# Expert rows filed by running order, and the first half of them loaded and summed during the last blocks: an encoder layer on one Trainium2 core

## The reference

```python
lg = xt @ w_rg + b_rg;  g_sel = top-1 group of 4           # 4 groups of 8 experts
le = xt @ w_re[g_sel] + b_re                               # scores of the 8 experts of that group
pe_top, e_sel = lax.top_k(softmax(le), 2)
gate = pg_top * pe_top / sum(pe_top)                       # two gates for each token
h = silu(xb @ w1[e]) * (xb @ w3[e])                        # xb: the token's normalised row
y = (h @ w2[e]) * gate
x = x + y_first + y_second                                 # both experts of a token
out = rmsnorm(x, final_norm_g)
```

## Time and profile before

| | |
|---|---|
| median of 3 runs | 1198.32 us (1197.93 to 1200.55) |
| span of the profiled execution | 1197.2 us |
| TensorE busy | 1093.9 us, 91% |
| VectorE, ScalarE, GpSimd busy | 520.2, 400.4, 190.7 us |
| moved by DMA | 308.89 MB, mean 258 GB/s |
| from the last block's store to the end | 1159.04 to 1197.2 us |

### The profile page before, as it was taken

The page is one execution under the profiler, slowest core; times in us unless marked ns, Lnnn a source line. Parts: engine busy times, 40 slices in busy tenths (PEclk is TensorE's granted clock), DMA queues, the critical chain, the costliest instruction groups (busy, mean ns, idle before and its releaser), DMA issues.

```text
span 1197.2 us, 15506 instructions
## 1 busy us (share of the span) xinstructions
PE 1093.9 (91%) x5142; PEld 659.8 (55%) x5142; DVE 520.2 (43%) x893; ACT 400.4 (33%) x629; POOL 190.7 (16%) x236
## 2 busy tenths in 40 slices
PE   5999999999999999999968999999998898999960
PEld 4888888888866667878854333333332333333320
DVE  5741512111038897463363535352443343341518
ACT  5421323222135665112214242424143324233232
POOL 0110011010100000000001323232323333231210
PEclk9999999999999999999987999999998999998985
DMA  8733331711350005557368899999999999999536
GB/s 305 282 122 116 114 123 44 292 57 45 139 210 12 1 1 176 176 192 306 123 270 353 353 421 420 419 420 419 421 415 420 421 420 420 419 420 419 218 157 258
DMA packets 69248, 308.89 MB, mean 258 GB/s; under 512 B 9024, under 2 KB 9152, under 8 KB 43872
## 3 DMA queue, kind: packets, MB, share of 16 engines
q1 hardware_dynamic: 56144, 273.86, 57.4%
q0 software_dynamic: 13072, 34.63, 7.5%
HBM read 278.57 MB, written 39.06 MB: 265 GB/s over the span
## 4 chain that ended last, share of the span: by engine, by line
PE 69%; DMA 15%; DVE 9%; ACT 3%; issue 3%; SPq 0%; DVEq 0%; ACTq 0%; POOLq 0%; POOL 0%
PE ps L872 18%; PE ps L584 13%; PE ps L585 13%; PE ps L586 13%; DMA rawe<-in_w 11%; PE ps L899 7%; DMA x_scratch<-x 2%; PE ps L862 1%; DVE cur13b L1671 1%; ACT prob L1003 1%; PE ps L881 1%; DVE att L1376 1%; DVE mx L1356 1%; DVE mx L1355 1%; DMA ya<-y_scratch 1%
## 5 line engine op out<-in xcount | busy, mean ns | idle before, releaser
L584 PE MATMUL ps<-whi,xTh 128*128 128x512 f32 x480 | 187.8, 391 | 14.0 <-DVE wlo L1231 14.0
L585 PE MATMUL ps<-wlo,xTh 128*128 128x512 f32 x480 | 187.5, 391 | 0.0
L586 PE MATMUL ps<-whi,xTl 128*128 128x512 f32 x480 | 187.4, 391 | 0.0
L872 PE MATMUL ps<-cur13a,xT 128*64 128x512 f32 x656 | 159.3, 630 | 2.0 <-DVE xT L1648 1.6
L1671 DVE COPY cur13a<-rawe 128x4096 f32 x31 | 71.1, 2294 | 189.1 <-DMA rawe<-in_w 119.7
L872 PE MATMUL ps<-cur13b,xT 128*64 128x512 f32 x656 | 147.8, 592 | 0.0
L899 PE MATMUL ps<-cur,hT 128*64 128x512 f32 x640 | 146.2, 598 | 0.0
L1200 ACT ACTIVATE cur<-rawe 128x4096 f32 x31 | 112.1, 3617 | 3.7 <-issue 1.4
L969 ACT ACTIVATE zst<-ps,rstd 128x512 f32<-128x512 f32 x60 | 40.8, 687 | 204.4 <-PE ps L586 198.0
L584 PEld LDWEIGHTS ps<-whi,xTh 128*128 128x128 f32 x480 | 90.6, 189 | 33.0 <-issue 14.0
L585 PEld LDWEIGHTS ps<-wlo,xTh 128*128 128x128 f32 x480 | 90.7, 189 | 18.8
(11 more groups left out here) (212 smaller groups left out, 1384.1 us busy)
## 6 DMA issues: line engine op xcount, KB each, us to landing
rawe<-in_w SPq DMA_DIRECT2D x96, 2048.0 KB, 25.9
raw<-in_w_in SPq DMA_DIRECT2D x20, 1024.0 KB, 8.0
z_scratch<-zst POOLq DMA_DIRECT2D x60, 256.0 KB, 2.3
gat<-z_scratch SPq DMA_DIRECT2D x12, 512.0 KB, 3.9
xn_scratch<-rrow POOLq DMA_DIRECT2D x6, 1024.0 KB, 5.6
ya<-y_scratch SPq DMA_DIRECT2D x6, 1024.0 KB, 10.8
raw<-in_w_out SPq DMA_DIRECT2D x4, 1024.0 KB, 6.8
xcol<-in_x_cols SPq DMA_DIRECT2D x6, 512.0 KB, 10.2
```

Of the source, the lines that this page charges most:

```text
L584: pe.matmul(out, ah, bh, start=first, stop=False)
L585: pe.matmul(out, ah, bl, start=False, stop=False)
L586: return pe.matmul(out, al, bh, start=False, stop=last)
L872: mm = pe.matmul(ps[0][u * CAP:(u + 1) * CAP, :], xT[:, c, h * CAP:(h + 1) * CAP], cur13[h][:, :, c * 512 + u * 256:c * 512 + u * 256 + 25 ...
```

## The change

The two rows of a token are filed by the order in which its experts run: `slote` holds the smaller and the larger of the two places, so k = 0 is the expert that runs first. The gates are put in the same order. A third number, `nb - 4`, is computed. SP, after the load of `x2t`, reads that number, waits until so many stores have landed, and loads the k = 0 rows of 128 tokens each (512 KB each) to five buffers `ye` beside `gf`; the sixth reuses the first buffer and waits until VectorE has used it (`s_c1`). VectorE adds these rows to `x2t` right after its loop over blocks (`combine_first`). After `s_md` SP loads only the k = 1 rows, and `combine` has one instruction instead of two.

```diff
+    slote = small("slote", [P, 2, NT])
-    nbi = small("nbi", [1, 2], I32)
+    nbi = small("nbi", [1, 3], I32)
...
-    ya = [at(f"ya{t}", RAW_O + t * 8 * KB, [P, 2, D]) for t in range(NT)]
+    ya = [at(f"ya{t}", RAW_O + t * 4 * KB, [P, D]) for t in range(NT)]
+    ye = [at(f"ye{s}", (124 + 4 * s) * KB, [P, D]) for s in range(5)]
...
             sp.dma_start(x2t[:, :, :], x2_d.rearrange("(t p) d -> p t d", p=P)).then_inc(s_x2l, 16)
+            early = sp.value_load(nbi[0:1, 2:3], min_val=NE - 4, max_val=NB - 4)
+            sp.wait_ge(s_ys, 16 * early)
             sp.dma_start(gf[:, :], A["final_norm_g"].rearrange("(a n) -> a n", a=1).partition_broadcast(P)[:, 0, :]).then_inc(s_gf, 16)
+            for t in range(NT):
+                if t == 5:
+                    sp.wait_ge(s_c1, 1)
+                sp.dma_start(ye[t % 5][:, :], y_d[t * P:(t + 1) * P, 0, :]).then_inc(s_g0[t], 16)
             sp.wait_ge(s_md, 1)
             for t in range(NT):
-                sp.dma_start(ya[t][:, :, :], y_d[t * P:(t + 1) * P, :, :]).then_inc(s_g1[t], 16)
+                sp.dma_start(ya[t][:, :], y_d[t * P:(t + 1) * P, 1, :]).then_inc(s_g1[t], 16)
...
-            link(dve.tensor_copy(sloti[:, :, :], slotf[:, :, :]))
+            dve.tensor_tensor(slote[:, 0, :], slotf[:, 0, :], slotf[:, 1, :], ALU.min)
+            link(dve.tensor_tensor(slote[:, 1, :], slotf[:, 0, :], slotf[:, 1, :], ALU.max))
+            link(dve.tensor_copy(sloti[:, :, :], slote[:, :, :]))
...
+            dve.tensor_scalar(nbi[:, 2:3], ends[0:1, NE - 1:NE], 1.0 / CAP, -4.0, ALU.mult, ALU.add)
...
-            link(dve.reciprocal(gates[:, 0, :], v6[:, 7, :]))
-            link(dve.tensor_tensor(gates[:, 1, :], gates[:, 0, :], v6[:, 3, :], ALU.mult))
+            link(dve.reciprocal(v6[:, 4, :], v6[:, 7, :]))
+            dve.tensor_tensor(v6[:, 0, :], slotf[:, 0, :], slotf[:, 1, :], ALU.is_lt)
+            dve.tensor_tensor(v6[:, 1, :], slotf[:, 0, :], slotf[:, 1, :], ALU.is_ge)
+            link(dve.tensor_tensor(v6[:, 5, :], v6[:, 4, :], v6[:, 3, :], ALU.mult))
+            for k in range(2):
+                dve.tensor_tensor(gates[:, k, :], v6[:, 4, :], v6[:, k, :], ALU.mult)
+                link(dve.tensor_tensor(v6[:, 6, :], v6[:, 5, :], v6[:, 1 - k, :], ALU.mult))
+                link(dve.tensor_tensor(gates[:, k, :], gates[:, k, :], v6[:, 6, :], ALU.add))
...
+            def combine_first(t):
+                dve.wait_ge(s_g0[t], 16)
+                dve.scalar_tensor_tensor(out=x2t[:, t, :], in0=ye[t % 5][:, :], scalar=gates[:, 0, t:t + 1],
+                                         in1=x2t[:, t, :], op0=ALU.mult, op1=ALU.add).then_inc(s_c1, 1)
...
             def combine(t):
                 dve.wait_ge(s_g1[t], 16)
-                link(dve.scalar_tensor_tensor(out=x2t[:, t, :], in0=ya[t][:, 0, :], scalar=gates[:, 0, t:t + 1],
-                                              in1=x2t[:, t, :], op0=ALU.mult, op1=ALU.add))
-                dve.scalar_tensor_tensor(out=x2t[:, t, :], in0=ya[t][:, 1, :], scalar=gates[:, 1, t:t + 1],
+                dve.scalar_tensor_tensor(out=x2t[:, t, :], in0=ya[t][:, :], scalar=gates[:, 1, t:t + 1],
                                          in1=x2t[:, t, :], op0=ALU.mult, op1=ALU.add).then_inc(s_c2, 1)
...
             dve.wait_ge(s_x2l, 16)
+            for t in range(NT):
+                combine_first(t)
+            dve.wait_ge(s_c1, NT)
```

More of the change, by code:

```diff
@@ L363, in hybrid_layer @@
         s_g1 = [sem(f"s_g1{t}") for t in range(NT)]
+        s_g0 = [sem(f"s_g0{t}") for t in range(NT)]
+        s_c1 = sem("s_c1")
         s_c2 = sem("s_c2")
```

## The result

The changed kernel takes 1192.82 us (median of 5, 1192.00 to 1194.07), the kernel before in the same session 1198.94 us (5 runs, 1197.93 to 1200.55). The ratio is 0.9948 (0.9936 to 0.9960): 6.1 us faster. I had forecast 1190.7 and 7.6 us. The profiled execution has a span of 1191.0 us and was itself measured at 1192.82 us, so 1.8 us lie outside the span.

A forecast was written before the change was run, and what follows sets the result against it. It saw the weight stream at 415 to 421 GB/s mid-loop and 35.7 us without block work at the end. 1197.2 - 9.3 + 1.1 + 0.6 = 1189.6 us span, plus 1.1 gives 1190.7; range 1188.6 to 1193.6.

The forecast's parts named there:

- the two rivals at 1192.4 and 1192.6: TensorE's first product: another low-clock stretch, 1192.4, chance 0.07; last but one store: waits for three or four additions, 1192.6, 0.08.
- The early loads and additions: During the last block: six loads and additions hidden, ending about 1156 us; without that cover they would cost 7.2 us.
- my rival for a late wait: Early loads on SP: the wait passes only with the last store, so loads queue behind it; 1200.1 us, chance 0.03.
- The end, -9.3: After the last store: fourth tile's addition 5.4 us earlier, one addition fewer on three tiles saves 3.96; bounds 8.6 to 10.1.
- the shorter pieces are no slower: Loads after the last store: 512 KB in 4 KB rows keeps the pace of `x2t`, 1.39 us each.
- The gates, +1.1: Ahead of the first block: eight more gate instructions delay it, all paid at the end; 1.1 us, bounds 0.8 to 1.4.
- the traffic that stops near 680 us: Early loop: DMA nearly dry (41 GB/s) while SP waits for ScalarE's w2 copy, so a late block delays stream and end.
- The minimum and maximum of the places, 0: Ahead of the first gather: 0.28 us more, hidden behind the later gates; 0.3 us if that cover were gone.
- GpSimd held by the early additions, +0.6: Last but one store: early VectorE additions hold GpSimd's index copy and indirect DMA; 0.6 us late, from 0 to 2.5.
- the copy and one further addition are waited for: Last but one store: these waits make it land about 1158 us, 0.6 to 1.0 us late.
- Outside the span, 1.1: Whole execution: the median of the runs lies 1.1 us above the profiled span.
- The rival on the clock: TensorE's first product: longer idle time brings another 3.4 us at half clock, losing 1.7 us; 1192.4 us, chance 0.07.

The follow-up runs named there:

- e2_late_loads: Changed kernel with the loads of the k = 0 rows also waiting for the last store, so nothing is loaded or added early: 1199.72 us.
- e4_k_major: Changed kernel with both scratch tensors laid out [k, token, 1024], so each load's rows lie one behind the other: 1191.37 us.
- e6_pairs: Changed kernel with the k = 1 rows loaded in three loads of 1 MB instead of six of 512 KB, same places in memory: 1193.12 us.
- e1_front_only: Changed kernel with filing and gates in running order, but everything loaded and added after the last store as before: 1199.61 us.
- e9_no_reorder: Changed kernel without the eight instructions that put the gates in running order, so gates can go to wrong rows: 1190.42 us.
- e10_warm: Changed kernel with one extra unused TensorE product behind the turning of the rows of block 0 and of block 1: 1189.59 us.
- e11_best_warm: Changed kernel with gate instructions behind the first columns' copy, scratch laid out [k, token, 1024], and two extra unused TensorE products: 1188.95 us.
- e3_gates_later: Changed kernel with all 13 gate instructions moved behind the copy of the first block's columns: 1191.01 us.
- e7_adds_twice: Changed kernel with six more unused VectorE additions behind the early ones, beside the last store: 1191.97 us.

## Why the prediction was right, and where it was off

The forecast was the likeliest case, and that case came: 1192.8 is inside the range of 1188.6 to 1193.6, and no rival's mechanism decided. It was 2.1 us too fast, though, and outside the 1189.4 to 1191.9 of the forecast itself; it lies in the part of the range that I had added for the two rivals at 1192.4 and 1192.6, which didn't happen. One term that was too large (0.6) hid part of the others. Term by term:

**The early loads and additions.** As forecast: issued from 1136.66 us, the wait for the 37th store met long before, six additions without a gap, done at 1157.8, ten us ahead of the first addition of a `ya`. `e2_late_loads` is the proof from the other side. With all loads behind the last store it is 35.5 us from the first of them to the end, as it was before (35.7), and the median is 1199.7; my rival for a late wait gave 1200.1. The whole gain is the cover.

**The end, -9.3: mis-sized.** It measured -8.2, outside my bounds of 8.6 to 10.1. The step that failed is "the shorter pieces are no slower": I took the pace of `x2t`, 1.39 us for each 512 KB. The pace was right (1.47 us a tile from the first to the fourth addition), the first landing was not: 4.64 us behind the issue instead of 3.5, so the fourth tile started at 9.05 instead of 7.8 us. The rows of `x2t` are 4 KB as well, but they lie one behind the other, while the k = 1 rows are 8 KB apart; the pieces have one size and another pitch. `e4_k_major` changes the layout and has 3.30 us (3.28 and 3.39 in the two other kernels with that layout, 4.55 to 4.98 in all with single tiles at the wide pitch), `e6_pairs` changes only the number of loads and still starts slowly. The rest of the term was right: from the fourth tile's addition to the end 18.46 us, 4.0 less than before, where I had 3.96.

**The gates, +1.1.** The stretch grew by 1.09, and all of it was paid, as argued from the traffic that stops near 680 us. In the changed kernel it nearly stops from 681 to 685 us (69 and 47 GB/s over 2 us each), two us after that of before. `e1_front_only` and `e9_no_reorder` show both the size and that a later first block is a later end. In the changed kernel's own profile, though, about half of the 1.09 would have come from the late gather even without the eight instructions, as worked out under `e9_no_reorder`; that the number fits is in part luck. Time gained at the start holds less well: of 1.7 us in the clock `e10_warm` has 0.7 left at the end of the loop, and `e11_best_warm`, whose first w2 product starts 3.6 us earlier than the changed kernel's when both are counted from the exponential, has 2.3 left. It goes where VectorE waits for weights from the DMA queue, after 817 us.

**The minimum and maximum of the places, 0.** The copy of the columns stood behind the gates, as forecast, and the gather was ready before. TensorE had turned the rows 0.6 us ahead of the copy, so this cover is thin; with the gates moved away (`e3_gates_later`) the gather is what the copy waits for.

**GpSimd held by the early additions, +0.6: it was 0.** The holding is there: the index copy took 1.01 us, against 0.18 before, and the indirect DMA 1.15 against 1.01. But from ScalarE's filling of `ystage` for the last block but one to that for the last it is 5.52 us as before (1153.67 to 1159.19, and 1151.72 to 1157.24), so the slack swallowed the 1.0. The bracket at 1159.19 names the store. By the longest landing time of the last two stores, 2.6 us, it was there at 1158.9, after TensorE's product (which ends at 1158.25) and before ScalarE's start, with 0.3 us to spare. The step that failed is "the copy and one further addition are waited for": the copy waited for one addition, and the indirect DMA for none, it only ran 0.14 us longer. The Trainium skill, page "SBUF — State Buffer", section "Who interferes with whom", had this right: the copy, which reads SBUF, waited for an addition with two inputs to end (the fourth ends at 1155.4, the copy at 1155.45), and the indirect DMA was hardly held. I should have taken its 0; `e7_adds_twice` shows the same at the last store, for 0.4 us.

**Outside the span, 1.1: it was 1.8.** I had compared a median with the span of another execution. The profiled execution's own time is 1.82 us above its span. That is +0.7. In every run on record the execution's time is 1.8 us above its span.

**What no term held, +0.9.** The router's exponential came 0.9 us later in this profile than in that of before, ahead of all that changed: 0.75 of it is there at those router scores already. Among the profiles here it lies between 639.1 and 640.7 us.

The sum: 1.1 (end) + 0.7 (outside) + 0.9 (ahead of the change) - 0.6 (GpSimd) = 2.1 us, the whole miss. In the second session the changed kernel was at 1191.0, so the 0.9 is within what the kernel does by itself.

**The rival on the clock.** It had 0.07, and it did not happen in the changed kernel: the idle time before the first product was 1.35 us there, shorter than the 1.64 of before and not 2.8 as I had written, because the later index list pushed the turning of the rows back too. That was luck: only 0.36 us of the 2.36 by which the list is later is what I had put there for the change. The clock fell in block 1's product instead of block 0's. In `e2_late_loads` and `e6_pairs` the list came early, TensorE waited 2.6 us for the gates, and the rival came true. I priced it at 1.7 us; the products took 2.9 more, and 2.5 were left at the loads. It came in two of the seven profiles that have the long gate chain in front and no extra product, so its 0.07 was low, as far as so few can say.

## What to carry to other kernels

Halves of rows that are fetched apart should be laid out apart: with the rows in one block behind the other, the same 512 KB were in use 1.3 us sooner than at twice the pitch, and a pace taken from a contiguous load doesn't show that. When work is moved under a last stretch, price the cover by undoing the move alone (all loads behind the wait: the whole gain was gone) and look for what it puts in front of the first block, for that is paid in full at the end. A few us are read from stretches between named instructions of two profiles; the medians of one kernel in two sessions were 1.8 us apart here, and a profile is of one execution, which was up to 2.5 us off its kernel's median.

## What the runs showed of the hardware that I had not expected

- Reads of 4 KB pieces at a pitch of 8 KB moved 262, 262, 197 and 213 GB/s in the second to fifth us after their issue, and 381 in the sixth; 4 KB pieces one behind the other moved 319, 397, 328 and 197, and 352 in the sixth; 8 KB pieces 131, 410, 426 and 426. Why both kinds of 4 KB pieces are slow in the fifth us and not after it is open.
- In each profile without extra products TensorE ran at the lower level of its clock in part of the first product of block 0 or of block 1, or of both. The first took 3.65 us after 0.78 to 1.35 us of idle time (five profiles, and then block 1's took 4.98 to 5.35), 5.35 after 1.28 to 1.72 (four profiles, and then block 1's took 3.65), and 6.54 after 2.58 and 2.61 (block 1's 5.33 and 5.34). The two sides overlap at 1.28, so idle time is not all that decides. An extra product of 1.02 us in each of two gaps kept both at 3.65 (`e10_warm`, `e11_best_warm`).
- A number read by SP from SBUF puts about 1 us between two DMA issues (1134.90 + 0.37 to 1136.25); in the kernel before there is 0.05 us between the same two.
- The index list is ready at 635.2 to 635.7 us in five profiles and at 637.2 to 638.0 in the other eight, though the instructions ahead of it are the same in all kernels but the one before. The two groups part at a product of the router ahead of the places (TensorE, L802), and the granted clock makes most of the difference: at full clock the product takes 1.95 us, and where the clock falls to its lower level inside it, 3.07 to 3.50. It also starts up to 1.4 us later there. `e6_pairs` and the changed kernel:

```profile
615.73 1.95 PE L802 MATMUL ps<-wrt,rT 128*128 128x36 f32 x16 [1.90 <-DVE lg L1523]
```

```profile
617.02 3.17 PE L802 MATMUL ps<-wrt,rT 128*128 128x36 f32 x16 [1.90 <-DVE lg L1523]
```

The list decides whether TensorE waits 1.1 to 1.7 or 2.6 us before its first product in a kernel with the long gate chain in front.
